# RMS norms: root and reciprocal, or one power of -0.5 on GpSimd

## What is computed

```python
def rms_norm(x, w):
    xf = x.astype(F32)
    y = xf * lax.rsqrt(jnp.mean(xf * xf, -1, keepdims=True) + NORM_EPS) * w.astype(F32)
    return y.astype(x.dtype)

def block(x, mods, nw, fw_in, fw_out, mixer, params, init_state):
    sh1, sc1, g1, sh2, sc2, g2 = mods
    h = rms_norm(x, nw[0]) * (1 + sc1) + sh1
    out, state = mixer(h, init_state, *params)
    x = x + g1 * out
    h = rms_norm(x, nw[1]) * (1 + sc2) + sh2
    x = x + g2 * swiglu(h, fw_in, fw_out)
    return x, state
```

## Time and profile before

| | us |
|---|---|
| median of 3 runs | 2961.81 |
| lowest, highest | 2957.46, 2971.84 |
| the profiled execution's own time | 2957.81 |
| span of that profile | 2956.0 |
| TensorE matmul busy | 2465.6 (83%) |
| VectorE busy | 1293.3 (44%) |
| ScalarE busy | 903.4 (31%) |
| GpSimd busy | 0.2 (0%) |
| mean granted TensorE clock | 0.903 of full |

### The profile page before, as it was taken

One profiled execution on the slowest core, in us unless ns is written; L12 is line 12 of the kernel. 1 busy time (PEld: TensorE's weight loads), 2 busy tenths in 40 slices (PEclk: granted clock), 3 DMA queues, 4 the chain that ended last, 5 costly groups with the idle time before them and its releaser, 6 DMA issues.

```text
span 2956.0 us, 51987 instructions
## 1 busy us (share of the span) xinstructions
PE 2465.6 (83%) x21424; PEld 2249.1 (76%) x21424; DVE 1293.3 (44%) x2212; ACT 903.4 (31%) x1697; POOL 0.2 (0%) x4
## 2 busy tenths in 40 slices
PE   4799579649996669999797699999985869999797
PEld 2799366238884459999797598888864869999796
DVE  1311644375565442222322477878874232221323
ACT  1322222213331132222212356555553132221311
POOL 0000000000000000000000000000000000000000
PEclk8899678569998789999899799999987989999898
DMA  5122424210001212222122133333330212222121
GB/s 199 50 72 77 142 72 171 92 32 7 3 3 58 78 40 67 76 73 76 52 70 96 39 100 98 94 98 97 93 111 22 64 36 71 78 71 76 54 70 49
DMA packets 319412, 216.46 MB, mean 73 GB/s; under 512 B 11640, under 2 KB 304902, under 8 KB 318854
## 3 DMA queue, kind: packets, MB, share of 16 engines
q1 hardware_dynamic: 260944, 179.66, 20.3%
q10 hardware_dynamic: 58294, 34.41, 3.9%
HBM read 205.74 MB, written 8.29 MB: 72 GB/s over the span
## 4 chain that ended last, share of the span: by engine, by line
PE 75%; DVE 18%; ACT 2%; issue 2%; DMA 1%; DVEq 1%; ACTq 1%; SPq 0%
PE bank L271 46%; PE bank L2022 10%; PE bank L494 2%; PE bank L1279 2%; DVE wide_low L289 1%; PE bank L2057 1%; DVE arena L1492 1%; ACT arena L487 1%; PE bank L412 1%; PE bank L1364 1%; PE bank L2061 1%; DMA ring<-in_mod_w_dram 1%; DVE ring_low L2111 1%; DVE rstd L505 1%; PE bank L1382 1%
## 5 line engine op out<-in xcount | busy, mean ns | idle before, releaser
L271 PE MATMUL bank<-narrow_high,w_split 128*128 128x320 f32 x4096 | 774.0, 311 | 80.9 <-DVE w_split L279 80.9
L271 PEld LDWEIGHTS bank<-narrow_high,w_split 128*128 128x128 f32 x4096 | 648.1, 189 | 81.9 <-issue 81.9
L279 DVE TENSOR_TENSOR w_split<-ring,w_split 128x1024 fp32r<-128x1024 f32 (+1 forms) x192 | 229.4, 1202 | 597.3 <-ACT w_split L276 588.4
L271 PE MATMUL bank<-narrow_low,w_split 128*128 128x320 f32 x2048 | 469.7, 311 | 0.0
L271 PE MATMUL bank<-wide_high,w_split 128*128 128x320 f32 x1920 | 371.3, 316 | 85.5 <-DVE w_split L279 85.5
L276 ACT ACTIVATE w_split<-ring 128x1024 fp32r<-128x1024 f32 (+1 forms) x192 | 198.9, 1042 | 754.5 <-PE bank L271 408.7
L271 PEld LDWEIGHTS bank<-wide_high,w_split 128*128 128x128 f32 x1920 | 310.5, 193 | 87.5 <-issue 87.5
L271 PEld LDWEIGHTS bank<-narrow_low,w_split 128*128 128x128 f32 x2048 | 345.7, 189 | 0.0
L271 PE MATMUL bank<-wide_low,w_split 128*128 128x320 f32 x960 | 223.9, 315 | 0.0
L2022 PE MATMUL bank<-x_high,pair_high 128*128 128x320 f32 x768 | 186.7, 325 | 30.0 <-DVE ring_low L2111 29.9
L1679 DVE TENSOR_TENSOR arena<-arena,bank 128x640 f32 (+1 forms) x44 | 36.1, 821 | 366.8 <-PE bank L271 366.8
(11 more groups left out here) (353 smaller groups left out, 2994.6 us busy)
## 6 DMA issues: line engine op xcount, KB each, us to landing
ring<-in_mod_w_dram SPq DMA_DIRECT2D x96, 512.0 KB, 4.7
ring<-in_ffn_w_in_dram SPq DMA_DIRECT2D x88, 512.0 KB, 3.8
ring<-in_od_w_in_dram SPq DMA_DIRECT2D x48, 512.0 KB, 4.1
arena<-cumulative_decays ACTq DMA_DIRECT2D x80, 256.0 KB, 3.5
ring<-in_ev_w_in_dram SPq DMA_DIRECT2D x32, 512.0 KB, 3.8
ring<-in_ffn_w_out_dram SPq DMA_DIRECT2D x32, 512.0 KB, 3.6
ring<-in_od_w_out_dram SPq DMA_DIRECT2D x16, 512.0 KB, 3.7
ring<-in_ffn_w_out_dram SPq DMA_DIRECT2D x16, 384.0 KB, 3.3
```

Of the source, the lines that this page charges most:

```text
L271: mm = E.matmul(twin[pr][:, b, :], w_split[:, ws, w, k, :], r(k)[:, b * HT:(b + 1) * HT], start=st and n == 0, stop=en and n == 2)
L279: return V.tensor_tensor(w_split[:, ws, 1, 0:kt], ring[:, s, 0:kt], w_split[:, ws, 0, 0:kt].bitcast(F32), ALU.subtract)
```

## The change

A column of `small` is set to -0.5 once, at the start of `stage_load`. In `stage_norm` the root on ScalarE and the reciprocal on VectorE are taken out. In their place `rstd`, whole rows of 640 tokens in all 128 partitions, is raised to the power of that column, spread along the row, by one instruction on GpSimd. GpSimd waits for `m_s` and raises `rt_s`; VectorE's wait for `rt_s` stays where it was. Stages may now have a fifth function, for GpSimd, and `stage_norm` has one (and an empty one for SyncE); GpSimd runs these one after the other, without fences. The rest of the kernel is the same.

```diff
         def dve(dve):
+            lv.done(V.memset(small[:, 11:12], -0.5))
             V.memset(rows[:, :, :], 0.0).then_inc(c_s, 1)
             lv.done(V.memset(cs_T[:, :, :], 0.0))
...
                 A.activation(sq[:, k % 2 if ring2 else k, :], src[:, k, :], ACT.Square).then_inc(sq_s, 1)
-            act.wait_ge(m_s, n0 + 1)
-            la.done(A.activation(rstd[:, :], rstd[:, :], ACT.Sqrt))
-            act.sem_inc(rt_s, 1)
             if shift_at is not None:
...
             lv.done(V.tensor_scalar(rstd[:, :], pairs[2][:, 0:T], 1.0 / (kt * P), EPS, ALU.mult, ALU.add))
             dve.sem_inc(m_s, 1)
             dve.wait_ge(rt_s, n0 + 1)
-            lv.done(V.reciprocal(rstd[:, :], rstd[:, :]))
             for k in range(kt):
...
-        return pe, act, dve
+        def pool(pool):
+            pool.wait_ge(m_s, n0 + 1)
+            nc.gpsimd.tensor_tensor(rstd[:, :], rstd[:, :], small[:, 11:12].to_broadcast([P, T]), ALU.pow).then_inc(rt_s, 1)
+
+        return pe, act, dve, lambda sp: None, pool
...
     @block.sync
     def _(sp):
         for st in stages:
-            if len(st) == 4:
+            if len(st) >= 4:
                 st[3](sp)
+
+    @block.gpsimd
+    def _(pool):
+        for st in stages:
+            if len(st) == 5:
+                st[4](pool)
```

## The result

Before, the median was 2962.85 us (2957.46 to 2971.84, 4 runs); with the change it is **3532.93 us** (3520.66 to 3536.06, 4 runs). The ratio is 1.1916, with a 95% interval of 1.1884 to 1.1949: 570 us slower. The range of the prediction ended at 3412 us.

What follows compares the result with a forecast made beforehand. Though TensorE was busy in 83% of the span, root and reciprocal were put on the path, 30.6 us in six norms. 6 x (26.0 - 4.93) plus 0.2 gave +126.6 us, forecast 3088 us, range 2963 to 3412 us.

Steps and rivals of the forecast that it cites:

- The place: Between mean and first scaling in each of six norms: root, reciprocal and waits alone on the path, 5.10 us each.
- The formula: Change over the six norms: 6 x (p - 4.93) us, p being the duration of one GpSimd power.
- The duration p: One GpSimd power of 128x640 in each norm: 26.0 us, as logarithm, product and exponential.
- the same 27 steps: Steps of one power: logarithm, product and exponential, counted from the kernel's own VectorE logarithm without its reciprocal; 26.0 us.
- The bound: Upper limit for one power: 27 steps, each as slow as the 4.15 us reciprocal, 112 us.
- The case of a slow program: Rival for the six powers: each step costs more than a pass, p from 60 to 112 us; chance 0.13.
- The sign: Whole kernel: slower by over 0.5%, chance 0.78.
- Handovers: Before and after each power, between VectorE and GpSimd: as today's, 0.10 + 0.07 = 0.17 us.
- Table loads at nothing: The root's four table loads of 1283 ns, costed at nothing: covered by TensorE's sums, five microseconds deep in the third norm.
- One pass of GpSimd, as a rival: In the six norms, a power streams like plain arithmetic, p from 0.8 to 2.46 us; chance 0.10.
- The first call: First GpSimd power: by the Trainium skill's rule about 6 us more, paid once; no run showed it.
- The longer pauses: TensorE's six pauses lengthen but cost no more clock than now: nothing either way.

Runs made afterwards that it cites:

- the third kernel: The kernel before with root and reciprocal replaced by one ScalarE instruction, the table function for the reciprocal root: 2930.83 us, ratio 0.9907.
- the first experiment: The kernel before with a list of GpSimd powers, products and sums of several sizes beside it on an idle tile: 2956.74 us, ratio 0.999.

## Why the prediction was wrong

- **The place, right.** It put the root and the reciprocal alone on the path, 5.10 us in each of six norms. The shortened stretch of the third kernel gave back 28 us where 25 were expected, and the changed kernel's difference lies in the six stretches (584.5 us, where the spans differ by 577.7).
- **The formula, right.** 6 x (p - 4.93) with the measured p = 102.33 gives +584, against 577.7 in the spans and 570 in the medians; the 14 us between are no term of the prediction and are not explained.
- **The duration p, wrong, and this is the step that failed.** "Giving the exponential a polynomial as long as the logarithm's, p = 12.6 + 0.8 + 12.6 = 26.0 us": it is 102.33, 3.9 times as much. The count priced GpSimd's steps at VectorE's pace of about 1.3 ns per column (0.824 us for 640); on GpSimd a power costs 159 ns per column, 124 such passes and not 27. The argument beside it, that a program would be cheaper by keeping intermediates in registers, pointed the wrong way. GpSimd's own pace explains a small part only: at its 2.0 ns per column for a product, in the first experiment, the same 27 steps would be some 35 us (an estimate from these rows). Whether a power has more steps or dearer ones, no run shows.
- **The bound, right, and the range cut inside it.** The upper bound, 27 steps at the reciprocal's pace, was 112 us, and 102 lies under it. The case of a slow program had a chance of 0.13 and the range stopped at p = 80, in its middle. The sign, to which the prediction gave 0.78, was right. No row showed the operation, and its engine had no arithmetic row at all; nothing in the rows made 26 us likelier than 100.
- **Handovers, right.** 0.15 and 0.04 us, 0.19 together where 0.17 was put.
- **Table loads at nothing, right, though the cover was not five microseconds everywhere.** The four of line 481 are gone and a fifth one, in front of the first Silu of the convolution stage, too. In the fourth norm the load ended at 2229.40, only 0.24 us before line 502 started; even there it was not waited for. The fifth one held up its Silu, but the third pair of Silus starts 8.60 us behind the start of ScalarE's last instruction of the stage before with the load, and 8.59 without it. Line 500 still waits for the sums on TensorE (12.51 us of idle time before it in the first norm), as line 502 did in the earlier trace rows. Where a load was put on the path, it cost 1.31 us.
- **One pass of GpSimd, as a rival.** The Trainium skill's figure (GPSIMD Engine Reference, Elementwise — side-by-side cycle accounting) is right for what it prices: 1.0 us for a product or sum of 512 columns here, 2.0 ns per column, against its 4497 ns for 2048, 2.2 ns. A power is another matter.
- **The first call.** The Trainium skill (GPSIMD Engine Reference, Instruction dispatch) has some 6 us for the first call of a freshly loaded kernel. The traces show none: in the changed kernel the first power is as long as the others and starts 0.15 us after the mean. A cost hidden in the 70 us before it is ruled out by the first experiment, where the first power starts at 1.97 us, 0.10 us behind the records that set GpSimd up (MODIFY_POOL_CONFIG), and its 81.92 us lie on the line of the other sizes.
- **The longer pauses, right within 1.4 us each.** The windows of the second norm of the changed kernel: the power, the scalings and the split, and the next stage's first and second 5 us.

```profile
1181.00:1283.00 102.00, 0.00 (x0) 0.00 (x0) 0.20 (x1) 0.00 (x0) 101.66 (x1) 0.51 0.00 0
1283.00:1300.00 17.00, 0.00 (x0) 0.00 (x0) 14.30 (x25) 15.06 (x27) 0.68 (x1) 0.50 0.00 0
1300.50:1305.50 5.00, 5.00 (x19) 5.00 (x20) 3.20 (x3) 0.83 (x1) 0.00 (x0) 0.50 0.00 0
1305.50:1310.50 5.00, 5.00 (x34) 5.00 (x33) 0.00 (x0) 0.11 (x1) 0.00 (x0) 0.94 0.00 0
```

The same 5 us in the kernel before:

```profile
1107.70:1112.70 5.00, 4.95 (x21) 4.96 (x22) 3.32 (x3) 0.95 (x1) 0.00 (x0) 0.59 0.00 0
```

After a pause of 120 us TensorE starts at the 1.2 GHz level as it did after one of 23 us. It did 19 matmuls in its first 5 us where before had 21, and rose in the second five. The 200th matmul behind this pause ended 0.8 us later than before, counted from the first; behind the pauses of the other four of the first five norms the difference lies between 1.4 us later and 1.3 earlier.

## What to carry to other kernels

An operation is priced by the engine that does it: the reciprocal root from ScalarE's table took one pass of 0.74 us for 640 columns, and the same function as a power on GpSimd took 102 us. On the path, ask for the price per column of the very operation, and if no row has it, let the range reach to the bound. GpSimd's power goes by columns alone, at 0.4 + 0.159 us each: at 28 columns it equals the root and reciprocal of this kernel's whole row, and off the path 310 us of it cost nothing here. Turning a replicated row into a few columns made the power cheap, but here the turning was paid on TensorE, whose sums took 17.2 us instead of 10.4 at a granted clock of 0.50.

## What was not expected of the hardware

- GpSimd's power takes the same time for 1 partition as for 128 (20.71 and 20.78 us for 128 columns) and, within 0.24 us, for every exponent tried, 1 included.
- 40 one-column matmuls with a weight load each (80 records of either kind, two for each) kept TensorE busy for 17.2 us and its granted clock stayed at 0.50, while the 16 wide ones of the kernel before (32 records) had 0.85 in the same place.
- The same scan was 9 us shorter in two of the kernels, with 14.6 us less at the lower clock, although nothing in it was changed.
- ScalarE's reciprocal root from PSUM, with scale and a bias column, took 0.79 us against 0.74 from SBUF without them.
